# A hybrid layer on one core: q, k, v projected before z, the delta rule's steps spread over more units, attention steps spaced further apart

## What is computed

```python
xn = rms_norm(h, attn_norm)
proj = xn @ w_in            # columns: gq gk gv gz | gb ga | mq mk mv
# group A, 8 heads of 128: gated delta rule
qkv = silu(causal_short_conv(concat[gq, gk, gv], conv_w))      # 4 taps
q, k = l2_norm(q) * 128**-0.5, l2_norm(k)
beta, g = sigmoid(gb), -exp(A_log) * softplus(ga + dt_bias)
# per chunk: decay from cumsum(g); A = strict((k*beta) @ k.T * decay)
# Tm = inverse(eye + A);  u = Tm @ (v*beta) ...;  state S goes on to the next chunk
o_A = rms_norm(o, norm_w) * silu(gz)
# group B, 8 heads of 128: causal softmax attention, q and k RMS-normed
h = h + concat(o_A, o_B) @ w_o
```

## Time and profile before

| | us |
|---|---|
| median of 3 runs | 1399.21 (1399.19 to 1400.61) |
| span of the profiled execution (the page gives no other time of its own) | 1398.9 |
| PE busy in it | 1361.3 (97%) |
| PE weight loads | 1159.9 (83%) |
| DVE busy | 784.0 (56%) |
| ACT busy | 621.2 (44%) |
| POOL busy | 72.3 (5%) |
| PE's share of the chain that ended last | 89% |

### The profile page before, as it was taken

How to read it: one execution, slowest core, us unless ns; L and a number is a source line. 1 busy time by engine, 2 the same in 40 slices (tenths; PEclk the granted TensorE clock), 3 DMA queues, 4 the chain that set the end, 5 groups by cost and what they waited for, 6 DMA issues and landing times.

```text
span 1398.9 us, 19058 instructions
## 1 busy us (share of the span) xinstructions
PE 1361.3 (97%) x7067; PEld 1159.9 (83%) x7067; DVE 784.0 (56%) x909; ACT 621.2 (44%) x776; POOL 72.3 (5%) x94
## 2 busy tenths in 40 slices
PE   5999999999999899999999999999999999999998
PEld 4799998887888778888888888888888888888886
DVE  5456667657656555555555555444455555455554
ACT  5454445334344454544444444333444444444442
POOL 3000003214300000000000000000000000000000
PEclk9999999999999999999999999999999999999999
DMA  7556564333332176666656665656666566555553
GB/s 223 169 161 197 168 196 150 101 97 119 92 91 91 60 270 196 187 194 191 183 183 194 193 189 185 194 195 195 193 187 193 180 196 187 187 181 189 191 193 134
DMA packets 129412, 240.43 MB, mean 172 GB/s; under 512 B 12819, under 2 KB 13126, under 8 KB 129350
## 3 DMA queue, kind: packets, MB, share of 16 engines
q1 hardware_dynamic: 129248, 239.56, 54.3%
q10 hardware_dynamic: 102, 0.03, 0.0%
HBM read 237.45 MB, written 2.10 MB: 171 GB/s over the span
## 4 chain that ended last, share of the span: by engine, by line
PE 89%; DVE 5%; ACT 2%; POOL 2%; issue 1%; DMA 1%; SPq 0%; DVEq 0%; ACTq 0%; POOLq 0%
PE pair L478 24%; PE pair L480 24%; PE pair L479 24%; PE bg L624 4%; PE pair L661 3%; PE pair L663 3%; PE pair L662 3%; DVE w_lo L1043 1%; PE bg L608 1%; ACT w_hi L776 1%; PE bg L713 1%; PE bg L514 1%; DMA h<-in_x_dram 1%; DMA raw<-in_w_o_dram 0%; POOL q_rs L396 0%
## 5 line engine op out<-in xcount | busy, mean ns | idle before, releaser
L1043 DVE TENSOR_TENSOR w_lo<-raw,w_hi 128x1024 fp32r<-128x1024 f32 x444 | 542.6, 1227 | 459.3 <-ACT w_hi L776 456.0
L776 ACT ACTIVATE w_hi<-raw 128x1024 fp32r<-128x1024 f32 x444 | 468.3, 1059 | 496.6 <-PE pair L480 443.9
L478 PE MATMUL pair<-w_hi,xT_hi 128*128 128x512 f32 x1088 | 433.2, 398 | 0.0
L480 PE MATMUL pair<-w_hi,xT_lo 128*128 128x512 f32 x1088 | 424.8, 390 | 0.0
L479 PE MATMUL pair<-w_lo,xT_hi 128*128 128x512 f32 x1088 | 424.1, 390 | 0.0
L480 PEld LDWEIGHTS pair<-w_hi,xT_lo 128*128 128x128 f32 x1088 | 204.5, 188 | 43.7
L478 PEld LDWEIGHTS pair<-w_hi,xT_hi 128*128 128x128 f32 x1088 | 204.8, 188 | 39.2
L479 PEld LDWEIGHTS pair<-w_lo,xT_hi 128*128 128x128 f32 x1088 | 204.9, 188 | 38.8
L478 PE MATMUL pair<-w_hi,actT_hi 128*128 128x512 f32 x352 | 137.7, 391 | 0.0
L480 PE MATMUL pair<-w_hi,actT_lo 128*128 128x512 f32 x352 | 137.1, 389 | 0.0
L479 PE MATMUL pair<-w_lo,actT_hi 128*128 128x512 f32 x352 | 137.0, 389 | 0.0
(11 more groups left out here) (216 smaller groups left out, 1048.2 us busy)
## 6 DMA issues: line engine op xcount, KB each, us to landing
raw<-in_w_in_dram SPq DMA_DIRECT2D x112, 512.0 KB, 3.7
raw<-in_w_gate_dram SPq DMA_DIRECT2D x88, 512.0 KB, 4.4
raw<-in_w_up_dram SPq DMA_DIRECT2D x88, 512.0 KB, 3.8
raw<-in_w_down_dram SPq DMA_DIRECT2D x88, 512.0 KB, 4.6
raw<-in_w_o_dram SPq DMA_DIRECT2D x32, 512.0 KB, 4.7
raw<-in_w_ple_gate_dram SPq DMA_DIRECT2D x32, 512.0 KB, 4.3
h<-in_x_dram SPq DMA_DIRECT2D x8, 512.0 KB, 6.6
raw<-in_w_ple_proj_dram SPq DMA_DIRECT2D x4, 512.0 KB, 5.0
```

The lines of the kernel that those rows point to most:

```text
L478: mm(banks[t][:], hi[:, ts], wh, start=first, stop=False)
L480: m = mm(banks[t][:], lo[:, ts], wh, start=False, stop=last)
L776: f(w_hi[j % RING][:], raw[j % RING][:], ACT.Copy).then_inc(hi_ready, 1)
L1043: v.tensor_tensor(w_lo[j % RING][:], raw[j % RING][:], w_hi[j % RING][:].bitcast(F32), ALU.subtract).then_inc(lo_ready, 1)
```

## The change

The q, k, v blocks come first (units 0 to 47), in the order q, k, v of heads 0 to 3, then q, k, v of heads 4 to 7; z is units 48 to 63; mix stays 64 to 111. The loops over q, k, v are written out instead of looping over three. The gates' columns ride on the second q, k, v block, and `ba` and `gc` stay in units 17 and 21. Delta steps are dealt over the second halves of blocks 3, 4 and 5 (units 28 to 31, 36 to 39, 44 to 47) and over units 52 to 111. The heads' scores start at units 103, 106, 109 and 112, with `pT` two units later and `pv` four.

```diff
-U_QKV, B_QKV = 2 * UPB, 2
-U_MIX, B_MIX = U_QKV + 6 * UPB, 8
+U_QKV, B_QKV = 0, 0
+U_Z, B_Z = 6 * UPB, 6
+U_MIX, B_MIX = U_Z + 2 * UPB, 8
...
+QKV_BLOCKS = [(kind, half) for half in range(2) for kind in range(3)]
...
-    slots = [(u, k) for u in range(U_MIX + LEAD, U_WO + 1) for k in range(2)]
+    slots = [(u, k) for n in range(3, 6) for u in range(n * UPB + 4, n * UPB + UPB) for k in range(2)]
+    slots += [(u, k) for u in range(U_Z + 4, U_WO) for k in range(2)]
...
-    for i, u in enumerate((U_WO - UPB, U_WO - UPB // 2, U_WO, U_WO + 2)):
+    for i, u in enumerate((U_WO - 9, U_WO - 6, U_WO - 3, U_WO)):
         for k in range(2):
             at[u][k].append(("sc", 2 * i + k))
-            at[u + 1][k].append(("pT", 2 * i + k))
-            at[u + 2][k].append(("pv", 2 * i + k))
+            at[u + 2][k].append(("pT", 2 * i + k))
+            at[u + 4][k].append(("pv", 2 * i + k))
...
                 if step == "q_tok":
-                    if b < 2:
-                        for q in range(2):
-                            wait_pair_read(pe, B_MIX - 2 + q)
-                    else:
+                    wait_pair_read(pe, B_QKV + 3 * hg + 2)
+                    if hg:
                         wait_read(pe, ("ogT", b - 2))
...
+                        if n == 1:
+                            ba = k_tile_ba(k, bk)
+                        if kk == KU - 1:
+                            last.then_inc(unit_used, 1)
+                        for s in AT[u][kk]:
+                            burst(s)
+                    if n == 2 and j in (1, 5):
                         burst(("ba" if j == 1 else "gc", 0))
...
-            straight(U_MIX, B_MIX, 6, UPB, lambda b, k: (xT_hi[:, k, :], xT_lo[:, k, :]))
+            straight(U_Z, B_Z, 8, UPB, lambda b, k: (xT_hi[:, k, :], xT_lo[:, k, :]))
...
-            for u in range(2 * UPB):
-                split(u + LEAD, u + LEAD)
-                if (u + 1) % UPB == 0:
-                    z_end(u // UPB)
-            split(U_QKV + LEAD, LEAD)
-            post("baT", 0)
-            qkv(0, True)
-            with act.Fori(1, 3) as i:
-                qkv(i, False)
+            split(LEAD, LEAD)
+            for n in range(6):
+                for j in range(UPB):
+                    u = U_QKV + n * UPB + j
+                    if j:
+                        split(u + LEAD, u + LEAD)
+                    for k in range(2):
+                        for s in AT[u][k]:
+                            post(*s)
+                    if n == 2 and j in (1, 5):
+                        post("ba" if j == 1 else "gc", 0)
+                if n == 1:
+                    post("baT", 0)
+                conv(n, U_QKV + (n + 1) * UPB + LEAD)
```

More of the change, by code:

```diff
@@ L324, in _ @@
                     sp.dma_start(h[:, t, half_cols], x_d[:, t, half_cols]).then_inc(x_landed[t], 16)
-            for j in range(2 * UPB):
-                load(j, j, w_in, KU * (j % UPB), C_Z + j // UPB * CB)
-                if j == RING - 1:
+            for u in range(U_Z):
+                kind, half = QKV_BLOCKS[u // UPB]
+                load(u, u, w_in, KU * (u % UPB), kind * HEADS * P + half * CB)
+                if u == RING - 1:
                     sp.dma_start(p_in[:], A["p"][0, 0].rearrange("(t p) n -> p t n", p=P)).then_inc(p_landed, 16)
@@ L333, in _ @@
                     sp.dma_start(wba_raw[:], w_in[:, :, C_BA:C_MOBA]).then_inc(ba_landed, 16)
-            with sp.Fori(0, 3) as i:
-                for j in range(2 * UPB):
-                    load(i * (2 * UPB) + (U_QKV + j), j, w_in, KU * (j % UPB), i * (2 * CB) + j // UPB * CB)
+            for j in range(2 * UPB):
+                load(U_Z + j, j, w_in, KU * (j % UPB), C_Z + j // UPB * CB)
             with sp.Fori(0, 3) as i:
@@ L1208, in _, with conv @@
             dve.wait_ge(small_landed, 48)
-            def conv(i, bl, u, j):
-                n = i * 2 + bl
+            def conv(n, u):
+                kind, half = QKV_BLOCKS[n]
                 done = 0
@@ L1215, in conv @@
                     if tap == 0:
-                        split(u, j)
+                        split(u, u)
                     sh = CONV - 1 - tap
                     for m in range(4):
-                        t0 = i * HEADS + (4 * bl + m)
+                        t0 = kind * HEADS + 4 * half + m
                         if tap == 2:
@@ L1244, in _ @@
-            for u in range(2 * UPB):
-                split(u + LEAD, u + LEAD)
-                if (u + 1) % UPB == 0:
-                    b = u // UPB
-                    for t in range(NT):
-                        dve.wait_ge(z_sig, 2 * b + t + 1)
-                        v.tensor_tensor(zg[:, t, b * CB:(b + 1) * CB], pair[b][t][:], sq[t][:],
-                                        ALU.mult).then_inc(pair_free[b], 1)
-            split(U_QKV + LEAD, LEAD)
-            qkv(0, True)
-            with dve.Fori(1, 3) as i:
-                qkv(i, False)
+                    t0 = kind * HEADS + 4 * half + 2 * q
```

106 lines of the change are left out of this document (42 added, 64 removed).

## The result

The changed kernel takes **1387.03 us** (median of 4 runs, 1385.52 to 1390.18), against 1399.8 (1399.19 to 1400.61) for the kernel before on the same chip: a ratio of 0.9908, 95% interval 0.9896 to 0.992. Forecast: 1387.6 us, 1381 to 1395. The profiled execution took 1385.52 us for a span of 1383.8; that of before had a span of 1398.9.

A forecast was written before the change was run, and what follows sets the result against it. TensorE, busy 97% of a 1398.9 us span, was taken as the bound, with 22.7 us of losses to win. 1398.9 - 22.7 + 3.4 + 7.0 + 0.3 + 0.4 + 0.3 = 1387.6 us, range 1381 to 1395.

The forecast's parts named there:

- Projections turned round: q, k, v and z units in the other order: same work for PE, POOL and transfers, so no gain.
- Delta steps spread: Units 64 to 103: steps dealt over 144 slots instead of 92; of 10.5 us lost by PE, 3.4 remain.
- Attention two units apart: Units 104 to 119: of 12.2 us lost by PE, 7.0 remain, including 3.2 at the last output transpose.
- the dip of 1.2 us: TensorE's clock falling to half behind the last output transpose's long wait, costing 1.2 us.
- Block ends: Convs at q, k, v block ends: delta work makes VectorE at most 1.15 us late, under 1.4 of room; cost 0.
- Gates 0.3: Gates moved behind a conv hold ACT 3.3 us; unit 21's weights come 0.3 us late.
- table loads 0: Four more table loads on ACT, ahead of an instruction that waits for DVE anyway: cost 0, bound 5.1 us.
- POOL 0.4: POOL's long products meeting tight splits on VectorE: 0.78 us for about half a clash, 0.4 us.
- B: Last output transpose doesn't wait, so 3.2 us and the dip vanish: 1383.2 us, or 1381; chance 0.20.
- C: VectorE over 1.4 us late to three convs at block ends, 1.5 to 3 us beyond each: 1392 to 1396; chance 0.13.
- D: Spacing does nothing for attention, since VectorE sets the pace; the 12.2 us stay: 1392.8 us; chance 0.08.
- E: Slower: the 8.3 us decay chain falls wholly behind a block end, needing 6.2 us late at three ends; chance 0.03.

The follow-up runs named there:

- order_only: The kernel before with only the projections turned round, delta and attention steps left where they were; 1399.08 us, ratio 0.9993.
- att_undone: The changed kernel with the attention steps back at their old units and distances; 1393.21 us.
- ends_late: The changed kernel with five extra sums on VectorE, 3 us in all, ahead of the conv's taps at the ends of blocks 2 to 5; 1389.6 us.
- wo_first: The changed kernel with the weights of W_O's second block issued ahead of the residual's slices; 1384.85 us, ratio 0.9887.

## Why the prediction held, by its steps

*Projections turned round, "nothing".* Right: order_only, 0.9993. (The pages list 94 instructions of POOL in both kernels, not 97.)

*Delta steps spread, 3.4 us remain of 10.5.* Right in direction, and better than forecast: 2.2 remain. The decay rows do not wait any more. Inside the term two sizes were off. The second output's transpose waits 1.17 us where I had 0.3 (its scaling begins behind a split and the q step, timeline of PE):

```profile
295.56 0.63 PE L611 MATMUL bg<-ident,V 128*128 128x128 f32 x4 [1.17 <-DVE V L1144]
```

The 3.1 us of short waits and passages between bursts measured 2.2 - 1.17 = 1.0, to the 0.3 of the count: a pass from burst to projection costs less than I had put down when nothing waits in it.

*Attention two units apart, 7.0 remain of 12.2.* Measured 5.5; without the dip of 1.2 us, which this execution doesn't have, the forecast is 5.8. The walk through VectorE's queue gave 3.2 us for the last transpose; the row says 2.90:

```profile
449.10 0.63 PE L611 MATMUL bg<-ident,V 128*128 128x128 f32 x4 [2.90 <-DVE V L1144]
```

W_O's wait, forecast 2.0, is 1.8. The dip of 1.2 us behind the long wait is not in the profiled execution (granted clock 1.00 in its window). The median seems to contain one: of the four executions the profiled one had a mean clock of 1.000 and a span of 1383.8, two had 0.998 and spans of 1385.2 and 1385.4, some 1.5 longer, and one 0.996 and 1388.5.

*The number.* That 1387.6 lies within 0.6 us of the median is in part luck. The sum starts from a span and gives a span, and the profiled one is 1383.8: 3.8 us less. The dip is 1.2 of this, the delta term 1.2, the attention term 0.3, the three additions 1.0. The median is nevertheless near, because 1.7 us of an execution pass outside its span, of which the forecast added nothing, and because most executions are some 1.5 us longer than the profiled one. The start was high as well: the profiled execution of before was a long one (last section).

*The sharing out.* What does not hold is how the gain was shared between the parts. The prediction priced spread and spacing as two terms, one for each stretch of units. The runs show that in units 104 to 119 neither does it alone: the spread gives 0 there, the spacing 2.1, both 6.5. The total doesn't hang on this, since the walk was made for the changed kernel as a whole; the sharing was stated without asking what one part does while the other is missing. A reader who had shipped half of the change by these terms (att_undone) would have expected about 5.2 us less gain, and got 6.2; one who had shipped only the spacing would have expected 5.2 us of gain, and got 2.3.

*Block ends, 0.* Right, and shown: all four stayed within their room. The walk had the worst of them 1.15 us late under a room of 1.4, so 0.25 us to spare; the trace leaves 0.5 and 0.6 us at units 44 and 52. It was close all the same: ends_late shows that what comes on top of that room is paid in full.

*Gates 0.3, table loads 0, POOL 0.4.* No wait of PE's falls in unit 21, though its weights come only 0.24 us ahead. ACT has 4 instructions more (780 for 776), the table loads, with no cost visible. Two splits were stretched beside POOL's products, to 1.72 and 1.37 us for a median of 1.23: 0.6 us of VectorE's time, and none of PE's. The kernel before has two as well (2.01 and 1.69 us), so the change brought no more of them. The prediction's reading of it as a cost at block ends (1.2 us, a time near 1388.8) did not come true, since neither split was one that PE waited for. By the Trainium skill (SBUF — State Buffer, "SBUF: two separate sides"), whichever of a VectorE instruction with two SBUF inputs and a GpSimd one starts first keeps the shared port for its whole length. The trace agrees: the two splits were stretched by products that had begun before them (118.10 and 149.01 us), and a product that began behind a split (146.91 us behind 146.68) took 2.15 us itself, for the 1.27 of the earlier trace rows. Shortest, median and longest of the splits in the changed kernel (the view of the tile w_lo):

```profile
L1029 DVE TENSOR_TENSOR w_lo<-raw,w_hi x444: 1210/1226/1718, 11.9 to 1367.8; 128x1024 fp32r<-128x1024 f32 x148
```

*What would show it.* Of the signs, these came: the decay rows and the probabilities' transposes don't wait, L611 waits 2.9 us at 449.10, and ACT waits 7.15 us for W_O's weights (7.16 before); no split at units 36, 44 or 52 is late, and units 64 to 103 lose under 4 us. One failed: the dip behind the long wait. And L611 waits twice, not once.

*Rivals.* B (the last transpose doesn't wait) fell with the 2.90 us row. C (block ends late) is refuted by the room, and ends_late shows its mechanism is real beyond 0.5 us. D (the spacing does nothing for attention) is wrong by att_undone: 6.2 us. E needed 6.2 us late at three ends, and none was late.

## What to carry to other kernels

When two kinds of wait stand in the same stretch of the bottleneck engine, price them together: removing one can hand its time to the other, and an experiment with one alone says little of what both are worth. To ask whether work may be put ahead of a deadline, read how long its product lies ready before it is taken; here the added work cost nothing up to that, and was paid in full beyond. A queue that issues a late-needed transfer before an early-needed one is worth looking for at every stage border: turning that order round gave some 2 us here with a few lines moved.

## What the runs showed of the hardware

Executions of one program differ in TensorE's mean granted clock, and with it in length. The changed kernel's four executions had mean granted clocks of 1.000, 0.998, 0.998 and 0.996, and spans of 1383.8, 1385.2, 1385.4 and 1388.5 us; with the same order of work and the same waits, the 2.90 us wait was followed by a dip in wo_first (granted clock 0.97 over 413 to 474 us, the four transposes behind it 1.08 us instead of 0.63) and by none in the profiled execution of the change. I had counted the dip as certain. A difference of 1.5 us between two profiled spans, or between the losses of one stretch in two traces, is thus no finding until the granted clocks agree.

The row of wo_first, timeline of PE:

```profile
449.00 1.08 PE L610 MATMUL bg<-ident,V 128*128 128x128 f32 x4 [2.90 <-DVE V L1143]
```

Outside the span an execution takes some 1.7 us (1385.52 for a span of 1383.8, 1389.37 for 1387.7), the same in every kernel here. The profiled span of before lay only 0.3 us under its median; with 1.7 us around it, it fits the longest of the three times shown (1400.61).
